# A hybrid trunk layer on one core: first norm summed by TensorE, filter network started earlier, one ScalarE table set for logarithm and exponential

## Chip, core and metric

The kernel runs on one core of a Trainium2 chip. The metric is the device time of one execution in microseconds (us). It is written for the engines directly: every engine has its own instruction queue, and semaphores order them. The profile calls TensorE's matmuls PE and its weight loads PEld, VectorE DVE, ScalarE ACT, GpSimd POOL and SyncE SP.

## What is computed

Two layers (DEPTH = 2) of a trunk, over 512 latent and 128 context tokens (T = 640 columns), with D_MODEL = 1024. The parts that the change touches:

```python
def _rmsnorm(x, w):
    xf = x.astype(jnp.float32)
    y = xf * lax.rsqrt(jnp.mean(xf * xf, axis=-1, keepdims=True) + EPS)
    return (y * w.astype(jnp.float32)).astype(x.dtype)

def _hyena_filters(seq, w1, b1, w2, b2, w3, freq):
    ...
    h = jnp.sin(fr * (z @ w1.astype(f32) + b1.astype(f32)))
    h = jnp.sin(fr * (h @ w2.astype(f32) + b2.astype(f32)))
    h = h @ w3.astype(f32)
    deltas = jnp.abs(jnp.linspace(HY_SLOW_DECAY, HY_FAST_DECAY, HY_W, dtype=f32))
    return h * jnp.exp(-t[:, None] * jnp.tile(deltas, 2))

def _trunk_layer(x, p, l, cond, ctx):
    ...
    h = _rmsnorm(x, p['norm_mix_w'][l]) * (1.0 + sc_a) + sh_a
    mix, new_ctx = _mixer_sublayer(h, p, l, ctx)
    x = x + gt_a * mix
    h = _rmsnorm(x, p['norm_mlp_w'][l]) * (1.0 + sc_m) + sh_m
    x = x + gt_m * (jnp.square(jax.nn.relu(h @ p['mlp_w1'][l])) @ p['mlp_w2'][l])
    return x, new_ctx
```

The mixer has four branches (latent attention A, gated delta rule B, Hyena long convolution C whose filters come from `_hyena_filters`, differential attention D). Each has further RMS or L2 norms. A final norm follows the second layer.

## The kernel before

The activations stay transposed in SBUF: `x` and `h` are 8 chunks (KC = 8) of 128 features by 640 tokens. Every 1024-wide product is split into a high and a low part: weights come by DMA into a ring of four slots (`w_ring`), ScalarE rounds them into `w_high` (`high_part`, `win_high`), GpSimd subtracts to get `w_low` (`low_part`), and TensorE multiplies high by high, high by low and low by high. The order on every engine is written out by hand.

**The start.** SyncE issues the loads of the condition, of the first constants, of `x`, of two blocks of the input projection, and then of four 2 MB groups of modulation weights (`w_early`, groups 0 to 3); group 2 waits for the first projection block, group 3 for the second. Projection blocks 2 and 3 are issued when groups 0 and 1 have landed. ScalarE squares the eight chunks of `x` into `h` (`square`). VectorE adds each squared chunk to the next, in a chain of seven adds. TensorE then sums over the partitions with a matrix of ones (`first_norm_sum`), and ScalarE makes the reciprocal root as exp(-0.5 ln(mean + eps)) (`root`). From there on `first_projection` goes through the four groups: `rows(g)` multiplies the condition by a group's weights, VectorE copies the result, `turn(g)` turns it into columns, VectorE forms scale and shift, then the chunks of `h` are scaled, split and multiplied into blocks 0 and 1 of the input projection (`high_products`, `low_products`).

**The filter network of layer 0.** It has three small products. `filter_first` multiplies positions by `w1`; VectorE reduces the argument to the sine's range in six instructions (`sin_arg(l, 1, ...)`), ScalarE takes the sine (`sine(1)`), TensorE multiplies by `w2` behind projection block 2, the same again (`sin_arg(l, 2, ...)`, `sine(2)`), and then `windowed` multiplies five tiles by `w3`, two tiles behind block 3 and three behind block 4; VectorE multiplies each by its window. Between these VectorE runs a short convolution of three instructions for every projection block (`conv`), and ScalarE evacuates each block from PSUM (`evac_conv`), which also rounds the weights of the block two later. All of this is in program order on each queue, so that a late sine argument holds what stands behind it.

**The copy of x.** `x`'s SBUF space is used for other data in the mixer, so GpSimd stores `x` to a DRAM tensor `x_kept` when all chunks have been scaled, and brings it back chunk by chunk in `merge`'s last eight steps, each as soon as the merged chunk is taken.

**ScalarE's tables.** Logarithm and exponential stand in different function tables as the program is built: there is an ACT_TABLE_LOAD ahead of the logarithm and another one ahead of the exponential in every root. A load is placed ahead of the last wait of the instruction that it serves. `stay_busy` gives TensorE 31 products without use while the roots of the layers' later norms are made.

## Time and profile before

| | us |
|---|---|
| median of 3 runs | 2681.46 (2676.06 to 2685.02) |
| profiled execution, its own time | 2686.07 |
| its span | 2684.3 |
| PE busy | 2565.2 (96%) |
| PEld busy | 2397.3 (89%) |
| DVE busy | 1533.7 (57%) |
| ACT busy | 981.1 (37%) |
| POOL busy | 695.6 (26%) |

The profiled execution is one of several, and 1.8 us of its time lie outside its span. A busy PE in this table counts a matmul from its start to its modelled end, at whichever clock it ran.

### The profile page before, as it was taken

Reading aid. Unit: us, or ns where it says so; the run is one execution under the profiler, and the core shown is the slowest. Engines: PE = TensorE matmul, PEld = TensorE weight load, DVE = VectorE, ACT = ScalarE, POOL = GpSimd, SP = SyncE. Lnnn points to the kernel's source line nnn. Section 1 sums busy time; section 2 is a strip of 40 time slices with the busy share of each in tenths; the row PEclk is TensorE's granted clock in tenths of the full one; section 3 lists DMA queues with packets and bytes.
Section 4 is the critical chain, followed back from the end, with each engine's and each line's share of the span. In section 5 each row is a group of like instructions: output and inputs, shape, how many; then the busy total and the mean of one; then the engine's idle time right before and its main releaser. Section 6 shows DMA issues by size and latency. Waiting matters only on the chain.

```text
span 2684.3 us, 53995 instructions
## 1 busy us (share of the span) xinstructions
PE 2565.2 (96%) x23046; PEld 2397.3 (89%) x23046; DVE 1533.7 (57%) x2507; ACT 981.1 (37%) x1590; POOL 695.6 (26%) x528
## 2 busy tenths in 40 slices
PE   6998999999999999999999989999999999999997
PEld 5788897999999999999987888878898998999997
DVE  6666634546676636355475675355565957355364
ACT  4251033334432534253442511443344226253352
POOL 2322122332244220211223311323222431211202
PEclk9999999999999999999999999999999999999999
DMA  9010011633333223223431100234332422122222
GB/s 360 31 56 3 3 50 68 196 109 105 109 132 122 67 91 110 88 94 97 143 140 32 48 3 3 70 132 131 116 112 96 167 81 71 64 86 75 82 73 79
DMA packets 74713, 248.21 MB, mean 92 GB/s; under 512 B 8948, under 2 KB 21412, under 8 KB 73200
## 3 DMA queue, kind: packets, MB, share of 16 engines
q1 hardware_dynamic: 71264, 220.32, 24.3%
q0 software_dynamic: 3216, 24.49, 2.5%
q8 instruction: 183, 3.00, 0.5%
q14 instruction: 50, 0.41, 0.1%
HBM read 227.56 MB, written 17.21 MB: 91 GB/s over the span
## 4 chain that ended last, share of the span: by engine, by line
PE 77%; DVE 12%; ACT 6%; issue 4%; DMA 1%; POOL 1%; DVEq 0%; ACTq 0%; SPq 0%; POOLq 0%
PE ps_dense L1067 29%; PE ps_dense L1075 13%; PE ps_aux L1067 4%; PE ps_dense L1984 4%; PE ps_dense L1750 3%; PE ps_dense L1988 2%; PE ps_aux L1514 2%; DVE rs L3126 2%; PE ps_dense L1831 1%; PE ps_aux L1807 1%; PE ps_aux L1500 1%; PE ps_dense L1819 1%; PE ps_aux L1466 1%; ACT w_high L2510 1%; ACT flow L2520 1%
## 5 line engine op out<-in xcount | busy, mean ns | idle before, releaser
L880 POOL TENSOR_TENSOR w_low<-w_ring,w_high 128x256 fp32r<-128x256 f32 (+1 forms) x338 | 538.9, 1610 | 1417.9 <-ACT w_high L2130 1406.2
L2130 ACT ACTIVATE w_high<-w_ring 128x1024 fp32r<-128x1024 f32 x198 | 210.0, 1061 | 368.7 <-PE ps_dense L1067 260.3
L1067 PE MATMUL ps_dense<-z_both,w_high 128*128 128x320 f32 x2048 | 312.5, 310 | 0.0
L1067 PEld LDWEIGHTS ps_dense<-z_both,w_high 128*128 128x128 f32 x2048 | 302.6, 188 | 2.1 <-issue 1.6
L1075 PE MATMUL ps_dense<-h_high,w_high 128*128 128x320 f32 x1024 | 240.7, 316 | 8.0 <-DVE x_res L3148 3.5
L3292 DVE SCALAR_TENSOR_TENSOR x_res<-ps_dense,mod,x_res 128x320 f32<-128x320 f32 (+2 forms) x192 | 72.6, 434 | 292.5 <-PE ps_dense L1067 292.5
L1075 PE MATMUL ps_dense<-h_high,w_low 128*128 128x320 f32 x1024 | 233.1, 309 | 0.0
L1075 PE MATMUL ps_dense<-h_low,w_high 128*128 128x320 f32 x1024 | 232.5, 308 | 0.0
L1067 PE MATMUL ps_dense<-h_high,w_high 128*128 128x320 f32 x864 | 206.1, 320 | 11.4 <-ACT h_high L2177 8.5
L1067 PE MATMUL ps_dense<-h_low,w_high 128*128 128x320 f32 x864 | 191.4, 313 | 0.3 <-DVE h_low L2681 0.3
L1075 PEld LDWEIGHTS ps_dense<-h_high,w_high 128*128 128x128 f32 x1024 | 168.3, 188 | 15.4 <-issue 13.2
L1075 PEld LDWEIGHTS ps_dense<-h_low,w_high 128*128 128x128 f32 x1024 | 171.2, 188 | 0.0
L1075 PEld LDWEIGHTS ps_dense<-h_high,w_low 128*128 128x128 f32 x1024 | 170.9, 188 | 0.0
L1067 PEld LDWEIGHTS ps_dense<-h_high,w_high 128*128 128x128 f32 x864 | 147.0, 193 | 25.3 <-issue 13.5
L1067 PE MATMUL ps_dense<-z_both,w_low 128*128 128x320 f32 x1024 | 160.6, 309 | 0.0
L1067 PEld LDWEIGHTS ps_dense<-z_both,w_low 128*128 128x128 f32 x1024 | 152.8, 188 | 0.0
L1067 PEld LDWEIGHTS ps_dense<-h_low,w_high 128*128 128x128 f32 x864 | 145.5, 192 | 0.9 <-DVE h_low L2681 0.5
L1067 PE MATMUL ps_dense<-h_high,w_low 128*128 128x320 f32 x864 | 145.2, 310 | 0.0
L3170 DVE TENSOR_REDUCE att_s<-ps_aux 128x1 f32<-128x640 f32 (+1 forms) x120 | 82.2, 713 | 92.5 <-PE ps_aux L1807 51.9
L1067 PEld LDWEIGHTS ps_dense<-h_high,w_low 128*128 128x128 f32 x864 | 131.9, 189 | 0.0
L1984 PE MATMUL ps_dense<-h_low,w_high 128*128 128x320 f32 x392 | 117.1, 310 | 0.0
L1984 PE MATMUL ps_dense<-h_high,w_high 128*128 128x320 f32 x336 | 102.6, 317 | 10.1 <-DVE flow L3438 10.0
(529 smaller groups left out, 5126.2 us busy)
## 6 DMA issues: line engine op xcount, KB each, us to landing
w_ring<-in_w_mlp SPq DMA_DIRECT2D x128, 512.0 KB, 3.5
w_ring<-in_w_late SPq DMA_DIRECT2D x64, 640.0 KB, 4.0
w_ring<-in_w_gate SPq DMA_DIRECT2D x64, 512.0 KB, 5.2
w_ring<-in_w_in SPq DMA_DIRECT2D x48, 512.0 KB, 3.3
w_ring<-in_w_out SPq DMA_DIRECT2D x16, 512.0 KB, 3.4
w_ring<-in_w_early SPq DMA_DIRECT2D x16, 512.0 KB, 3.3
arena<-in_w_early SPq DMA_DIRECT2D x3, 2048.0 KB, 16.5
arena<-in_dft POOLq DMA_DIRECT2D x2, 2944.0 KB, 13.4
```

The source lines that it names most:

```text
L880: last = g.tensor_tensor(w_low[:, n % 2, k:k + step], ring[:, slot, k:k + step, :], w_high[:, n % 2, k:k + step].bitcast(F32), ALU.subtract)
L1067: last = mm(out[:, s, 0:HALF], w_[:, par_, k, :], x_[:, k, s * HALF:(s + 1) * HALF], start=first, stop=final)
L1075: last = mm(out[:, s, 0:HALF], w_[:, par_, k, :], x_[:, k, s * HALF:(s + 1) * HALF], start=k == 0 and x_ is x_high and w_ is w_high, stop= ...
L1466: return mm(psA[to, 2 * i, u * 64:(u + 1) * 64], lt[s % 3][rows(r), d, hh, rows(r)], mv, start=True, stop=True)
L1514: last = mm(out, wm[i][at, u], mv, start=not moved, stop=True)
L1750: last = mm(out[:, s, 0:HALF], w_[:, k, :], x_[:, k, s * HALF:(s + 1) * HALF], start=n == 0 and k == 0, stop=n == 2 and k == 1)
L1984: mm(out, w_[:, k // 2, k % 2], src[:, k], start=fresh and k == 0 and n == 0, stop=False, skip_group_check=True)
L1988: last = mm(out, rest[:, k // 2, k % 2], b_high[:, k], start=False, stop=k == 3, skip_group_check=True)
L2130: a(w_high[:, n % 2], ring[:, j, 0:KC, :], ACT.Copy).then_inc(w_high_in.sem, 1)
L3126: link(v.scalar_tensor_tensor(out=product, in0=w[:, a:b], scalar=1.0, in1=cond_c[:, a:b], op0=ALU.mult, op1=ALU.mult, accum_out=total))
L3170: v.tensor_reduce(small_[:, 2 * m, u:u + 1], src, AX.XY if len(src.shape) == 3 else AX.X, ALU.max, negate=True).then_inc(negmax.sem, 1)
L3292: last = v.scalar_tensor_tensor(out=dst[:, p:q], in0=ps, scalar=gate[:, s:s + 1], in1=dst[:, p:q], op0=ALU.mult, op1=ALU.add)
```

## The change

It has four parts. (1) VectorE sums the squared chunks 0 to 5 only; TensorE adds chunks 6 and 7 and the sum in its accumulation, after 12 products without use that start when `x` has landed. (2) `filter_first` of layer 0 goes ahead of the products of chunks 6 and 7, its three small loads are issued by GpSimd when `rows(0)` is done (before: `rows(1)` done and group 3 landed), and in layer 0 the second sine argument and the second sine go ahead of convolution 1 and of the evacuation of block 2. (3) In layer 0 `x_kept` is not written, and `x` comes back from the kernel's input. (4) A table set that holds logarithm and exponential is loaded by name in every root (`both_tables`), and the separate load ahead of the exponential is gone. `stay_busy` has 28 products.

```diff
-        squares_in = signal("squares_summed", 2 * (KC - 2), KC - 1)
+        squares_in = signal("squares_summed", 2 * (KC - 2), KC - 3)
...
-        x_out = signal("x_kept_out", 1, 0, 16)
+        x_out = signal("x_kept_out", 1, -1, 16)
...
-            held(pool, block_done.sem, RING + 2 * RING)
-            held(pool, ring_in[1].sem, 32)
+            held(pool, block_done.sem, RING + RING)
             filter_positions()
             first_par = ins["par"][DEPTH - 1]
             for a, b in ((PAR["w1"][0], PAR["w3"][0]), (PAR["lam"][0], PAR_W)):
                 pool.dma_start(par[:, a:b], first_par[:, a:b]).then_inc(z_in.sem, 16)
+            held(pool, ring_in[1].sem, 32)
...
-                held(pool, *x_scaled.nth(l, KC))
-                pool.dma_start(x_kept, x[:]).then_inc(x_out.sem, 16)
+                if l:
+                    held(pool, *x_scaled.nth(l, KC))
+                    pool.dma_start(x_kept, x[:]).then_inc(x_out.sem, 16)
...
-                    pool.dma_start(x[:, d], x_kept[:, d]).then_inc(x_back.sem, 16)
+                    pool.dma_start(x[:, d], (x_kept if l else ins["x"])[:, d]).then_inc(x_back.sem, 16)
...
             def first_norm_sum():
-                pe.wait_ge(squares_in.sem, KC - 1)
-                for a, b in SEGS:
-                    last = mm(psD[:, 0, a:b], c_("ones"), h[:, KC - 1, a:b], start=True, stop=True)
+
+                pe.wait_ge(x_in.sem, 16)
+                for _ in range(12):
+                    mm(psA[:, 2, 0:P], c_("ones"), c_("ones"), start=True, stop=True)
+                for n, (c, event) in enumerate(((KC - 2, x_squared.nth(0, KC - 1)), (KC - 1, x_squared.nth(0, KC)),
+                                                (KC - 3, (squares_in.sem, KC - 3)))):
+                    pe.wait_ge(*event)
+                    for a, b in SEGS:
+                        last = mm(psD[:, 0, a:b], c_("ones"), h[:, c, a:b], start=n == 0, stop=n == 2)
                 last.then_inc(sumsq_done.sem, 1)
...
-                for _ in range(31):
+                for _ in range(28):
                     mm(psA[:, 2, 0:P], c_("ones"), c_("ones"), start=True, stop=True)
...
+                pe.wait_ge(first_scale.sem, 2 * RING)
+                filter_first(0)
                 high_products(KC - 2)
                 high_products(KC - 1)
                 for b in range(2):
                     low_products(KC - 2, b)
                     low_products(KC - 1, b).then_inc(block_done.sem, 1)
-                    if b == 0:
-                        filter_first(0)
...
+            def both_tables():
+
+                nc.scalar.preload_act_table_set("natural_log_exp_and_others")
+
...
-                        nc.scalar.preload_act_table(ACT.Ln)
+                        both_tables()
...
-                    if n == 2:
+                    if n == 1 + (l > 0):
                         sine(2)
...
                 evac_conv(l, 11)
+                both_tables()
                 length_ln(l, 2)
...
             def diff_root(l):
 
+                both_tables()
                 act.wait_ge(*do_sum.nth(l, 1))
...
             a(cond_t[:], cond[:], ACT.Tanh, scale=0.5).then_inc(g_tanh.sem, 1)
+            both_tables()
             act.wait_ge(x_in.sem, 16)
...
-                    if n == 2:
+                    if n == 1 + (l > 0):
                         sin_arg(l, 2, flat, p_("hb2", r), r)
                     conv(l, n, dst, w, bias)
                     if n == 3:
                         dve.wait_ge(const_rest_in.sem, 48)
-                        dve.wait_ge(*x_out.nth(l, 1))
+                        if l:
+                            dve.wait_ge(*x_out.nth(l, 1))
                         dve.wait_ge(*dft_in.nth(l, 1))
...
-            for c in range(1, KC):
+            for c in range(1, KC - 2):
```

TensorE's first rows in the program, before: the sum over the partitions (L1113), the condition by weight group 0 (L1101), its turn (L1171).

```order
L1113 MATMUL ps_dense<-h_norm,con_and_par 128x512
L1113 MATMUL ps_dense<-h_norm,con_and_par 128x128
L1101 MATMUL ps_aux<-arena,cond_pad 32x128 x32
L1171 MATMUL ps_aux<-con_and_par,bout 128x8
L1101 MATMUL ps_aux<-arena,cond_pad 32x128 x32
```

The same place in the changed program, where L1115 are the products without use and L1120 the sum.

```order
L1115 MATMUL ps_aux<-con_and_par 128x128 x12
L1120 MATMUL ps_dense<-h_norm,con_and_par 128x512
L1120 MATMUL ps_dense<-h_norm,con_and_par 128x128
L1120 MATMUL ps_dense<-h_norm,con_and_par 128x512
L1120 MATMUL ps_dense<-h_norm,con_and_par 128x128
L1120 MATMUL ps_dense<-h_norm,con_and_par 128x512
L1120 MATMUL ps_dense<-h_norm,con_and_par 128x128
L1102 MATMUL ps_aux<-arena,cond_pad 32x128 x32
L1178 MATMUL ps_aux<-con_and_par,bout 128x8
```

Two sums and the 12 products stand ahead of what was the first row. The next place is on VectorE, between the first sine argument and the second one; before, with the end of the first argument (L2710), the convolutions 0 and 1 (L2692 to L2696, twice) and the start of the second argument (L2702).

```order
L2710 TENSOR_SCALAR arena<-arena 64x640
L2692 TENSOR_SCALAR arena<-stage,con_and_par 128x642
L2694 SCALAR_TENSOR_TENSOR arena<-stage,con_and_par,arena 128x642
L2696 SCALAR_TENSOR_TENSOR arena<-stage,con_and_par,arena 128x642
L2692 TENSOR_SCALAR arena<-stage,con_and_par 128x642
L2694 SCALAR_TENSOR_TENSOR arena<-stage,con_and_par,arena 128x642
L2696 SCALAR_TENSOR_TENSOR arena<-stage,con_and_par,arena 128x642
L2702 TENSOR_SCALAR arena<-ps_aux,con_and_par 64x640
```

And in the changed program, where the lines of the argument are L2718 to L2726 and those of the convolution L2708 to L2712.

```order
L2726 TENSOR_SCALAR arena<-arena 64x640
L2708 TENSOR_SCALAR arena<-stage,con_and_par 128x642
L2710 SCALAR_TENSOR_TENSOR arena<-stage,con_and_par,arena 128x642
L2712 SCALAR_TENSOR_TENSOR arena<-stage,con_and_par,arena 128x642
L2718 TENSOR_SCALAR arena<-ps_aux,con_and_par 64x640
```

Convolution 1 now stands behind the second argument. The third place is ScalarE's start; before, with the condition's tanh (L2615), the squares (L2142), the first rounded weights (L2622) and the root (L2155, L2156).

```order
L2615 ACT_TABLE_LOAD
L2615 ACTIVATE cond_t<-cond_s 128x16
L2142 ACTIVATE h_norm<-x_res 128x640 x8
L2622 ACTIVATE w_high<-w_ring 128x1024 x2
L2155 ACT_TABLE_LOAD
L2155 ACTIVATE rs<-ps_dense,con_and_par 128x640
L2156 ACT_TABLE_LOAD
L2156 ACTIVATE rs<-rs 128x640
```

And now, where L2108 is the load by name.

```order
L2630 ACT_TABLE_LOAD
L2630 ACTIVATE cond_t<-cond_s 128x16
L2108 ACT_TABLE_LOAD
L2153 ACTIVATE h_norm<-x_res 128x640 x8
L2638 ACTIVATE w_high<-w_ring 128x1024 x2
L2166 ACTIVATE rs<-ps_dense,con_and_par 128x640
L2167 ACTIVATE rs<-rs 128x640
```

One load has moved ahead of the squares, and the other one is gone.

## Rows read from the trace of the kernel before

**Rows 1.** The page's chain of work that ended last.

```profile
PE 77%; DVE 12%; ACT 6%; issue 4%; DMA 1%; POOL 1%; DVEq 0%; ACTq 0%; SPq 0%; POOLq 0%
```

**Rows 2.** Timeline of the start: start us, us, engine line op, [idle before <-releaser].

```profile
10.92 5.12 ACT L2142 ACTIVATE h_norm<-x_res 128x640 f32<-128x640 f32 x8 [8.28 <-DMA x_res<-in_x]
12.32 6.74 DVE L3526 TENSOR_TENSOR h_norm<-h_norm 128x640 f32<-128x640 f32 x7 [9.26 <-ACT h_norm L2142]
...
19.20 2.47 PE L1113 MATMUL ps_dense<-h_norm,con_and_par 128*128 128x512 f32 x4 [19.20 <-DVE h_norm L3526]
...
21.61 2.68 PE L1101 MATMUL ps_aux<-arena,cond_pad 128*32 128x128 f32 x64
21.72 0.79 ACT L2155 ACTIVATE rs<-ps_dense,con_and_par 128x640 f32<-128x640 f32 x1 [2.48 <-PE ps_dense L1113]
...
28.39 0.53 PE L1067 MATMUL ps_dense<-h_high,w_high 128*128 128x320 f32 x2 [1.34 <-ACT h_high L2177]
```

**Rows 3.** Timeline: what tells when the weight groups had landed.

```profile
18.83 5.26 SPq L790 DMA_DIRECT2D w_ring<-in_w_in  x2
...
35.15 0.54 POOL L892 DMA_DIRECT2D arena<-in_dft  x1 [11.41 <-DMA bout<-in_w_early]
...
38.37 1.95 PE L1101 MATMUL ps_aux<-bout,cond_pad 128*32 128x128 f32 x64
```

**Rows 4.** Timeline at the first filter product (L1136).

```profile
47.65 1.29 PE L1136 MATMUL ps_aux<-arena,con_and_par 33*64 33x512 f32 x4
47.75 0.44 ACT L2108 ACTIVATE stage<-ps_dense 128x320 f32<-128x320 f32 x1 [2.44 <-PE ps_dense L1067]
...
48.45 1.07 ACT L2130 ACTIVATE w_high<-w_ring 128x1024 fp32r<-128x1024 f32 x1
...
49.07 0.94 DVE L2702 TENSOR_SCALAR arena<-ps_aux,con_and_par 64x640 f32<-64x640 f32 x1 [2.75 <-PE ps_aux L1136]
...
49.58 0.56 PE L1067 MATMUL ps_dense<-h_high,w_high 128*128 128x320 f32 x2
```

**Rows 5.** Timeline from the second filter product (L1257) to the last tiles (L1246).

```profile
56.80 1.29 PE L1257 MATMUL ps_aux<-arena,con_and_par 64*64 64x512 f32 x4
...
61.76 0.93 DVE L2702 TENSOR_SCALAR arena<-ps_aux,con_and_par 64x640 f32<-64x640 f32 x1
...
68.01 0.74 ACT L2183 ACTIVATE arena<-arena 64x640 f32<-64x640 f32 x1 [5.58 <-DVE arena L2710]
...
68.89 3.75 PE L1246 MATMUL ps_aux<-con_and_par,arena 64*128 64x512 f32 x4 [3.58 <-ACT arena L2183]
...
74.60 0.69 DVE L2722 TENSOR_TENSOR arena<-ps_aux,arena 128x512 f32<-128x512 f32 x1
...
82.13 2.84 PE L1246 MATMUL ps_aux<-con_and_par,arena 64*128 64x512 f32 x6
```

**Rows 6.** Busy time by stretch: PE, PEld, DVE, ACT, POOL, PE's granted clock, DMA, GB/s.

```profile
72.60:77.70 5.10, 5.10 (x20) 5.10 (x20) 4.77 (x8) 0.00 (x0) 0.48 (x1) 0.50 0.00 0
```

**Rows 7.** The second instruction of a convolution, both layers: duration ns min/median/max, starts.

```profile
L2694 DVE SCALAR_TENSOR_TENSOR arena<-stage,con_and_par,arena x24: 886/889/3120, 55.6 to 1508.6; 128x642 f32<-128x642 f32 x24
```

**Rows 8.** The norm ahead of layer 0's MLP, and all loads ahead of a root's exponential.

```profile
L2156 ACT ACT_TABLE_LOAD  x5: 1283/1283/1283, 22.5 to 2672.4; - x5
...
893.91 1.24 PE L1119 MATMUL ps_dense<-h_norm,con_and_par 128*128 128x512 f32 x4
...
897.25 7.09 PE L1128 MATMUL ps_aux<-con_and_par 128*128 128x128 f32 x62
...
905.16 0.53 PE L1067 MATMUL ps_dense<-h_high,w_high 128*128 128x320 f32 x2 [0.82 <-ACT h_high L2177]
```

**Rows 9.** Timeline: what waits for differential attention's root in layer 0.

```profile
754.20 0.83 PE L1750 MATMUL ps_aux<-con_and_par_reused,w_proj_high 128*128 128x320 f32 x4 [0.54 <-issue]
```

**Rows 10.** Timeline: the first gate's tanh in layer 0's attention.

```profile
465.02 0.70 ACT L2363 ACTIVATE stage<-ps_dense 128x640 f32<-128x640 f32 x1 [1.71 <-PE ps_dense L1101]
```

**Rows 11.** The line that brings x back (L1038), min/median/max of both layers' 16 transfers.

```profile
DMA to landing us min/median/max: 3.2/3.3/5.0
```

More of the change, by code:

```diff
@@ L2443, in mla @@
                 act.wait_ge(*stored.nth(l, 1))
+                both_tables()
                 for n, wd in enumerate((256, 128)):
@@ L2602, in mlp_group @@
                 if at_end:
-                    nc.scalar.preload_act_table(ACT.Ln)
+                    both_tables()
                     for m in (KC - 2, KC - 1):
@@ L2615, in _ @@
             a(cond_t[:], cond[:], ACT.Tanh, scale=0.5).then_inc(g_tanh.sem, 1)
+            both_tables()
             act.wait_ge(x_in.sem, 16)
```

## The prediction

> **What bounds the kernel now.** I read the page first: TensorE carries 77% of the chain that ended last, VectorE 12%, ScalarE 6% [rows 1]. So an edit on another engine counts only where TensorE waits for it, and I looked at the four kinds of places that the change touches. At the start TensorE has nothing until 19.20, when VectorE's seven adds are through; its sum takes 2.47 and the weight rows begin at 21.61 [rows 2]. In the filter network of layer 0 TensorE stands 3.58 for the second sine, and then runs slowly [rows 5]: its granted clock is 0.50, the 1.2 GHz level, until 77.7 [rows 6]. In every norm outside the mixer ScalarE's logarithm, load and exponential are in series with TensorE, which has only idle products [rows 8]. In the mixer TensorE mostly works beside the roots.
>
> **The start.** Removed: two adds of the seven, 6.74/7 = 0.96 each, so the sum of chunks 0 to 5 is there at 12.32 + 5 x 0.96 = 17.1 instead of 19.1. Added: 12 products without use and two sums. TensorE can begin at about 10.95, when x has landed [rows 2]. One idle product takes 7.09/31 = 0.23 at full speed [rows 8], so 12 take 2.8, or 5.5 at half speed: they end by 16.5 at the latest, and the square of chunk 6 is there at about 15.4, that of chunk 7 at 16.0. A sum takes 1.24 where TensorE is warm [rows 8] and took exactly twice that, 2.47, in this place [rows 2]; the 64 weight rows behind it took 2.68 against 1.95 later [rows 2, 3], so the clock rose among them, after some 4 us of work. Starting 8 us earlier, the clock should rise within the 12 products. Then three sums of 1.24 end at about 19.3; were all at half speed, they would end at 16.5 + 3 x 2.47 = 23.9. Before it was 21.67. The load ahead of the first exponential (1.28) is gone too [rows 8], so the reciprocal root comes earlier by more than the sum does, and is not what comes last.
>
> The gain of 2.4 meets the DMA. Group 0 had landed at 18.83, group 1 at about 18.83 + 5.26 = 24.1 or just before, since these issues wait for them; group 3 at 35.15 [rows 3]. The rows of group 0 go from 19.3 to 21.3, those of group 1 from 24.0 to 25.9, and the first products of block 0 follow at 25.9 instead of 28.39 [rows 2]: 2.5 earlier. The last group's rows then come up at 38.37 - 2.5 = 35.9, 0.7 behind their landing [rows 3]. The three small loads that GpSimd now issues before group 3 is in can eat that 0.7, hardly more. I take **-2.5**, with ends -3.2 (down to the landing at 35.15) and +2.2 (all sums at half speed).
>
> **The filter of layer 0.** Moving `filter_first` ahead is not free. Its product takes 1.29, and block 0 was evacuated at 47.75, just as that product began [rows 4]; now block 0 ends behind it, and ScalarE's evacuation and the rounding of block 2's weights (48.45 to 49.52) move by about 1.2. TensorE began block 2 at 49.58, right on them [rows 4], so it begins block 2 at 50.8: **+1.2** (bounds +0.6 and +1.3). What it buys: VectorE waited 2.75 for the first argument [rows 4] and now starts it at about 46.4, so the first sine is no danger for the second product, which comes 7.2 behind block 2's start (56.80 against 49.58 [rows 4, 5]), at 58.0, ending at 59.3. The second argument, now ahead of convolution 1, starts at 59.4 instead of 61.76, and the sine ended 6.99 after the argument's start (61.76 to 68.75 [rows 5]). It ends at 66.4 at the latest. TensorE comes from block 3 at 65.3 + 1.3 = 66.6 (it stood 3.58 before 68.89 [rows 5]). So the wait is gone, and with it the low clock: two tiles took 3.75 and take 2.84 x 2/3 = 1.9 warm [rows 5]. Block 4 lasted from 72.6 to 82.1, 9.5, and at full speed it takes what block 2 took, 7.2 [rows 4, 5, 6]. TensorE is done with block 4 at 66.6 + 1.9 + 7.2 = 75.7 instead of 82.13: -6.4, with the 1.2 in it.
>
> What is late next is VectorE: it windowed the first tile at 74.60 [rows 5] with the convolutions 2 and 3 behind the sine, 6.6 after 68.01, and now has convolution 1 there too: three instructions of at most 0.89, so 2.7, or 4.9 if one of them is held as the longest here, 3.12 [rows 7]. From 65.7, the start of the new sine, this gives 65.7 + 6.6 + 2.7 = 75.0 to 77.2 for the first tile, and twice 0.69 more for the second. TensorE wants the second at about 76.7. I put 0.7 on it (bounds 0 and 3). Net **-5.7**; ends -7.0 and -2.5. The evacuation of block 2 behind the second sine (65.7 + 0.7) leaves block 4's weights 2 us to be rounded and ready by 68.5, enough.
>
> **No copy of x in layer 0.** 2.6 MB less to DRAM in a stretch where VectorE's wait for it is ahead of the first tile; before, the sine was later than the copy. Cost and gain 0 here; without this part the filter's gain could be held by it. The way back is from another DRAM tensor with the same shape and the same number of transfers, 3.3 each [rows 11]: 0.
>
> **Table loads.** Each root outside the mixer loses one load of 1.283 and a gap of about 0.02, in series: two norms ahead of MLPs, layer 1's first norm, the final norm. The first of the kernel is counted above. The cover is long enough: 28 idle products end 3 x 0.23 = 0.7 earlier, and the first real product comes 1.3 earlier than 905.16, where it stood idle for 0.82 [rows 8], so 0.2 of idle remains. 4 x 1.30 = **-5.2**, bounds -5.2 and -3.5. In the mixer: behind the scan's inputs one load goes ahead of the exponential and one comes back ahead of the next tanh, 0; at the roots of the scan and of latent attention TensorE works beside them, 0; a load comes in ahead of the first gate's tanh, but ScalarE stood there for 1.71 [rows 10], more than 1.28, so 0 (1.3 if that cover were gone). At differential attention's root TensorE stood 0.54 before the product that waits for the exponential [rows 9], which ends 1.28 earlier, twice in the kernel: up to -1.1, and I take **-0.5**, since VectorE and GpSimd bound that stretch next.
>
> The Trainium skill ("ScalarE: Activation LUTs", section "What ACT_TABLE_LOAD costs") puts a switch at about 2.66: the load and a drain of 1.38 behind it. In this trace the next instruction starts within 0.02 of the load's end, so the trace does not show the drain. By the page the four loads would be worth 10.6 in place of 5.2, and the sum 5.4 more.
>
> **The sum.** -2.5 - 5.7 - 5.2 - 0.5 = -13.9. Against the profiled execution, 2686.07, that is 2672.2. The median of the three runs is 4.6 lower than it, 2681.46, and I forecast the new median from there: 2681.5 - 13.9 = **2667.6**.
>
> **The rivals.** (a) *TensorE stays slow at the start*: the clock rises late, or falls again in the 2 us between the turn of group 0 and the landing of group 1 (it fell around the wait of 3.58, and did not fall at 1.34 [rows 2, 5]). Then the start gives between +2.2 and -1, the total about -10: 2671. (b) *The filter's gain goes into the next wait*: the tiles wait for VectorE for 3 us or more, and where the wait is long enough the clock falls there. Then the filter gives -2.5 or less, the total -8 to -10: 2672. (c) *A table switch costs more than its row shows* (the page's rule, worked out as a mechanism here: a pause of 1.4 in ScalarE behind each load): nothing in the trace shows it; 2662. (d) *Slower*: `in_x` is read more slowly than `x_kept`. GpSimd issues these loads one behind the other and waits for each, with the subtraction for the next block queued behind the wait, and TensorE behind that. The loads took 3.3 [rows 11], hidden in the step of a gate. It decides when one takes longer than a step of some 9 us; with 12 us each, 8 x 3 = 24 less 13.9 gives 2692. Nothing speaks for it, the sizes are the same. (e) *The filter part doesn't do what it says*, because the second argument waits for TensorE's second product in any case; that is true from 55 to 59.4, but the argument still starts 2.4 earlier and has no convolution ahead. Covered by (b).
>
> **Chances.** Forecast, all parts about as summed (2663 to 2671): 0.60. (a) 0.15, (b) 0.16, (c) 0.04, (d) 0.02, and 0.03 for a new median that moves by more than the parts do, since the three runs shown lie 9 us apart. The range, 2660 to 2675, holds the forecast, (a), (c) and most of (b). A measurement tells this kernel from no change at about 0.3%, 8 us, which is 2673.4: faster by more than that 0.82, within 0.3% 0.15, slower 0.03.
>
> **What would show it.** In the changed profile: TensorE busy from about 11; sum done at about 19.3, with the last sums near 1.24; weight rows of group 1 straight at the landing, near 24; block 0's first products near 26; no wait of over 1 us for ScalarE's sine, and a granted clock of 1.00 through 65 to 80 at both tile groups; a wait of about 1 us at the start of block 2. 7 loads fewer in all, none between a root's logarithm and its exponential, and TensorE's first product behind each norm 1.3 nearer to its sum. The prediction is wrong if the sums run at half speed, if the second tile group waits for VectorE for more than 3 us, or if the norms' products don't move with the exponential.

## The result, and the profile after

The changed kernel takes 2660.58 us, median of 4 runs (2659.78 to 2663.39); the kernel before, on the same chip, 2678.76 (2675.22 to 2685.02, 4 runs). The ratio is 0.9928 with a 95% interval of 0.9907 to 0.9949: 19.3 us less, between 13.7 and 24.9; the medians lie 18.2 apart. Forecast were 13.9 less. The changed kernel's time lies 0.6 inside the lower edge of the range (2660 to 2675), 7.0 under the forecast of 2667.6. The profiled execution took 2661.06, with a span of 2659.2 against 2684.3 before.

The page of the changed kernel, the chain of work that ended last, its shares by engine (the view of [rows 1]), and from the list of DMA queues the one that brings instructions:

```profile
PE 79%; DVE 10%; ACT 5%; issue 3%; DMA 1%; POOL 1%; SPq 0%; DVEq 0%; ACTq 0%; POOLq 0%
...
q8 instruction: 183, 3.00, 0.5%
```

VectorE's and ScalarE's shares fell by 2 and 1 points, and so did "issue".

Timeline of the start of the changed kernel, TensorE alone (start us, us, line, form, idle before and what ended it; the view of [rows 2]):

```profile
10.84 4.28 PE L1115 MATMUL ps_aux<-con_and_par 128*128 128x128 f32 x24 [10.84 <-DMA x_res<-in_x]
15.27 3.51 PE L1120 MATMUL ps_dense<-h_norm,con_and_par 128*128 128x512 f32 x12 [0.15 <-ACT h_norm L2153]
18.71 1.95 PE L1102 MATMUL ps_aux<-arena,cond_pad 128*32 128x128 f32 x64
...
23.58 3.34 PE L1102 MATMUL ps_aux<-arena,cond_pad 128*32 128x128 f32 x64 [2.04 <-DMA arena<-in_w_early]
26.85 0.79 PE L1068 MATMUL ps_dense<-h_high,w_high 128*128 128x320 f32 x2
```

The sums run at full speed (3.51 for three, 1.17 each) and end at 18.8, 0.5 ahead of the forecast. Then TensorE waits 2.04 for the second group of weight rows, and those rows take 3.34 where the first group's took 1.95. The stretches of the same profile say why (busy time of PE, PEld, DVE, ACT, POOL, then PE's granted clock, DMA share, GB/s); the second row is where the filter's first tiles are multiplied (the view of [rows 6]):

```profile
24.00:27.20 3.20, 3.20 (x58) 2.82 (x50) 2.23 (x7) 2.38 (x4) 0.00 (x0) 0.50 1.03 416
65.00:72.00 7.00, 7.00 (x40) 5.62 (x39) 6.89 (x5) 1.77 (x4) 5.25 (x2) 1.00 0.23 75
```

The clock had gone to 0.50, the 1.2 GHz level, right behind the wait. Block 0's first products come at 26.85, 1.54 earlier than before and not 2.5. That is this profile: in the changed kernel's second one (e12 below) the same wait is 1.40, the clock stays up, the rows take 1.95, and block 0 comes at 25.59:

```profile
23.71 1.95 PE L1102 MATMUL ps_aux<-arena,cond_pad 128*32 128x128 f32 x64 [1.40 <-DMA arena<-in_w_early]
25.59 0.56 PE L1068 MATMUL ps_dense<-h_high,w_high 128*128 128x320 f32 x2
```

The filter network in layer 0, same timeline and columns (the views of [rows 4, 5]):

```profile
43.18 1.29 PE L1143 MATMUL ps_aux<-arena,con_and_par 33*64 33x512 f32 x4
49.46 0.56 PE L1068 MATMUL ps_dense<-h_high,w_high 128*128 128x320 f32 x2 [1.27 <-ACT w_high L2141]
56.68 1.29 PE L1264 MATMUL ps_aux<-arena,con_and_par 64*64 64x512 f32 x4
65.14 1.98 PE L1253 MATMUL ps_aux<-con_and_par,arena 64*128 64x512 f32 x4
...
74.75 1.12 PE L1253 MATMUL ps_aux<-con_and_par,arena 64*128 64x512 f32 x2 [0.41 <-DVE arena L2741]
76.15 1.55 PE L1253 MATMUL ps_aux<-con_and_par,arena 64*128 64x512 f32 x3 [0.27 <-DVE arena L2741]
```

The wait of 3.58 is gone, the tiles take 1.98 for 3.75, and the price of the moved product stands where it was put: 1.27 of idle time ahead of block 2.

The norm ahead of layer 0's MLP, all engines (the view of [rows 8]):

```profile
877.15 6.42 PE L1135 MATMUL ps_aux<-con_and_par 128*128 128x128 f32 x56
877.36 0.79 ACT L2166 ACTIVATE rs<-ps_dense,con_and_par 128x640 f32<-128x640 f32 x1 [1.44 <-PE ps_dense L1129]
878.18 0.74 ACT L2167 ACTIVATE rs<-rs 128x640 f32<-128x640 f32 x1
...
883.78 0.39 PE L1068 MATMUL ps_dense<-h_high,w_high 128*128 128x320 f32 x1 [0.21 <-ACT h_high L2188]
```

The exponential starts 0.03 behind the logarithm, and the first product comes 6.63 behind the first idle one (877.15 to 883.78); before it was 7.91. That is the load, 1.28, and the idle rest is the 0.2 that was forecast.

### The profile page after: what moved, and what is told of

Same layout as the page of the kernel before. It is cut to its first block, busy times and chain, and to the rows that moved or that the text cites. A ratio compares the mean times of both kernels' runs of the same rounds, so it can differ in the third digit from the quotient of the medians.

```text
span 2659.2 us, 54007 instructions
## 1 busy us (share of the span) xinstructions
PE 2559.3 (96%) x23060; PEld 2391.8 (90%) x23060; DVE 1530.1 (58%) x2505; ACT 972.3 (37%) x1583; POOL 693.0 (26%) x527
## 4 chain that ended last, share of the span: by engine, by line
PE 79%; DVE 10%; ACT 5%; issue 3%; DMA 1%; POOL 1%; SPq 0%; DVEq 0%; ACTq 0%; POOLq 0%
PE ps_dense L1068 29%; PE ps_dense L1076 14%; PE ps_dense L1991 5%; PE ps_aux L1068 5%; PE ps_dense L1757 3%; PE ps_dense L1995 2%; PE ps_aux L1521 2%; PE ps_dense L1838 1%; PE ps_aux L1814 1%; PE ps_aux L1507 1%; PE ps_dense L1826 1%; DVE rs L3143 1%; PE ps_aux L1473 1%; ACT flow L2535 1%; ACT w_high L2525 1%
## 5 line engine op out<-in xcount | busy, mean ns | idle before, releaser
L1068 PEld LDWEIGHTS ps_dense<-h_high,w_low 128*128 128x128 f32 x864 | 132.0, 189 | 0.0
## 6 DMA issues: line engine op xcount, KB each, us to landing
arena<-in_w_early SPq DMA_DIRECT2D x3, 2048.0 KB, 18.2
```

What stands on the lines that cost most here:

```text
L1068: last = mm(out[:, s, 0:HALF], w_[:, par_, k, :], x_[:, k, s * HALF:(s + 1) * HALF], start=first, stop=final)
```

## Where the rest came from: pauses in TensorE's instruction stream

I followed the same instructions through both profiles. Behind the filter (TensorE's first product with 32 output rows, at 92.12 before, at 85.28 now; from here on the milestone) the changed kernel was 6.8 ahead; the two scans of the delta rule (branch B) I had not priced at all. I measure a scan from the product that always stands behind a pause of 1.17 to 1.19 (L1356; L1363 now) to the first product of `ps_dense<-stage,bout`, in before from 179.52 to 315.96 in layer 0 and from 1506.83 to 1639.56 in layer 1. These stretches in before, in the changed kernel, and in the kernel before profiled a second time (columns as above; layer 0, then layer 1):

```profile
179.52:315.96 136.44, 121.23 (x3009) 113.06 (x3009) 90.61 (x145) 28.76 (x52) 26.49 (x30) 0.96 0.04 11
1506.83:1639.56 132.73, 119.12 (x3008) 111.31 (x3008) 90.44 (x145) 28.76 (x52) 26.48 (x30) 0.97 0.04 11
```

```profile
172.66:300.29 127.63, 115.71 (x3009) 108.15 (x3009) 90.31 (x145) 28.89 (x52) 26.52 (x30) 1.00 0.04 11
1483.76:1615.84 132.08, 119.58 (x3009) 111.76 (x3009) 90.47 (x145) 28.89 (x52) 26.51 (x30) 0.97 0.04 11
```

```profile
178.73:311.47 132.74, 118.40 (x3008) 110.05 (x3008) 90.48 (x145) 28.75 (x52) 26.53 (x30) 0.99 0.04 11
1499.55:1632.47 132.92, 119.42 (x3008) 111.62 (x3009) 90.50 (x145) 28.76 (x52) 26.52 (x30) 0.97 0.04 11
```

The work is the same, 3009 products, and layer 0's took 8.8 less. Two things differ: how often the granted clock fell (3 times in 179 to 316 before, never in the changed kernel, once in the second profile), and pauses in the middle of a run of equal products, which wait for nothing that the profile shows. One of them in before, the same place in its second profile, and in the changed kernel, where the 64 products run through (timeline, TensorE alone):

```profile
291.67 1.59 PE L1514 MATMUL ps_aux<-arena 64*64 64x64 f32 x47
294.12 0.68 PE L1514 MATMUL ps_aux<-arena 64*64 64x64 f32 x17 [0.86 <-issue]
```

```profile
289.92 0.68 PE L1514 MATMUL ps_aux<-arena 64*64 64x64 f32 x17 [1.14 <-issue]
```

```profile
278.60 2.06 PE L1521 MATMUL ps_aux<-arena 64*64 64x64 f32 x64
```

What these pauses have in common shows when one counts. TensorE's products (x) from the start to just before two of them in the kernel before:

```profile
0.00:236.00 236.00, 203.66 (x2116) 177.60 (x2116) 151.74 (x233) 87.43 (x145) 67.79 (x56) 0.97 0.34 127
0.00:245.20 245.20, 211.57 (x2368) 184.90 (x2368) 158.15 (x244) 89.68 (x148) 71.08 (x59) 0.97 0.32 123
```

A product is two instructions (the weight load and the multiplication), and a wait that doesn't fit into one is an instruction of its own: 57 such waits stand ahead of the first pause, 65 ahead of the second. So the pauses stand at instruction 2 x 2116 + 57 = 4289 and 2 x 2368 + 65 = 4801: 512 apart, both 193 over a multiple of 256. The changed kernel's whole program has 2 x 23060 + 886 = 47,006 such instructions (before: 2 x 23046 + 886); in 3.00 MB of instruction traffic that is 64 bytes each, and a packet, 3.00 MB / 183 = 16 KB, holds 256. The runs below confirm that this queue is TensorE's and a packet 256 of its instructions: with 512 more instructions ahead (e7, e8) it has 185 packets, with 192 more (e10) 184, with 64 more (e9) still 183. In all 17 profiles of this study every pause inside the scans of over 0.25 us, 80 of them, stands 192 or 193 over a multiple of 256 (two counted 195). The packets themselves agree: ahead of each of the twelve pauses in the two profiles of before one had landed, and the products went on 1.19 to 1.50 after it (for the one above, landed at 292.93, products at 294.12). In all 80 it is 1.19 to 1.77. So a pause is not at a place in the algorithm but at a place in the packet; my reading, which fits all of this but which no run shows apart, is that TensorE there runs through short products faster than the packets come. Code put in ahead moves all later pauses to other products. The change puts 64 instructions ahead of layer 0's scan (12 idle products and 4 more sums, of two passes each); 12 of them are taken back at each of the two norms between the scans (3 idle products of two passes), so it is 40 in layer 1.

## The experiments

Fifteen runs follow; e5 is the kernel before and e12 the changed kernel, unchanged. A table first, from their profiles: "shift" is by how many instructions TensorE's code stands further than in before (modulo 256), then pauses of over 0.25 and their sum, falls of the clock, and the length of the scan.

| profile | layer 0: shift | pauses, sum | falls | us | layer 1: shift | pauses, sum | falls | us |
|---|---|---|---|---|---|---|---|---|
| before | 0 | 4, 3.33 | 3 | 136.4 | 0 | 2, 1.77 | 2 | 132.7 |
| e5 (before again) | 0 | 4, 2.77 | 1 | 132.7 | 0 | 2, 1.22 | 2 | 132.9 |
| e2 (filter) | 0 | 4, 3.02 | 1 | 132.7 | 0 | 2, 1.97 | 2 | 133.6 |
| e1 (tables) | 0 | 4, 3.03 | 1 | 133.2 | -24 | 3, 3.38 | 0 | 132.7 |
| e7 | 512 = 0 | 3, 1.51 | 1 | 130.9 | 0 | 3, 2.19 | 2 | 134.1 |
| e8 | 512 = 0 | 3, 2.34 | 1 | 132.0 | -24 | 5, 3.92 | 1 | 134.0 |
| e10 | 256 = 0 | 3, 2.09 | 2 | 133.5 | -24 | 4, 3.29 | 0 | 132.2 |
| e4 | 48 | 1, 0.37 | 0 | 128.4 | 48 | 4, 2.89 | 1 | 132.0 |
| e6 | 48 | 3, 1.18 | 1 | 130.7 | 48 | 3, 1.82 | 1 | 131.2 |
| changed | 64 | 0 | 0 | 127.6 | 40 | 3, 1.53 | 2 | 132.1 |
| e12 (changed again) | 64 | 0 | 1 | 129.4 | 40 | 3, 1.89 | 1 | 131.5 |
| e13 | 64 | 2, 0.60 | 0 | 127.9 | 40 | 3, 1.76 | 1 | 131.3 |
| e15 | 64 | 1, 1.17 | 1 | 131.1 | 40 | 3, 1.56 | 2 | 132.1 |
| e3 (start) | 64 | 1, 0.28 | 1 | 129.2 | 64 | 1, 0.36 | 1 | 129.1 |
| e9 | 64 | 2, 1.27 | 1 | 130.5 | 64 | 1, 0.62 | 1 | 129.4 |
| e11 | 64 | 0 | 0 | 127.6 | 64 | 1, 0.36 | 1 | 128.8 |
| e14 | 64 | 0 | 0 | 128.0 | 64 | 2, 1.51 | 0 | 129.0 |

Median of layer 0: 132.7 at a shift of 0 (7 profiles), 128.6 at 64 (8): 4.1 less. Of layer 1: 133.2 at 0 (4), 131.8 at 40 (4), 129.1 at 64 (4). The expectations below count a scan from a later product, 10.0 behind mine in layer 0 and 5.7 in layer 1: their 122 is 132 here. Each profile is of one execution, and not always of a middle one: e6's and e10's were the slowest of their 12.

**The three parts alone, and 12 idle products alone.** e1, e2 and e3 are the kernel before with the lines of the diff that belong to the tables (with the 28 idle products), to the filter, or to the first norm. e4 is the kernel before with

```
             def first_norm_sum():
+                pe.wait_ge(x_in.sem, 16)
+                for _ in range(12):
+                    mm(psA[:, 2, 0:P], c_("ones"), c_("ones"), start=True, stop=True)
```

> The kernel before with only the table part of the change (one table set for logarithm and exponential, 28 idle products for 31). By my sum: four norms give 1.30 each and the roots of differential attention up to 1.1, -5.7 in all, -4 to -6.5. Theory P (what the whole change gained beyond the sum lies in layer 0's mixer, in falls of TensorE's clock and pauses of its instruction stream that depend on where its code stands and when it runs, not in a part): -5.7 outside the mixer, and in the mixer of layer 0 the same number of clock falls and pauses as before, since no TensorE instruction is added ahead of it. Rival S (the tables part is worth more than its rows, by a pause of 1.4 behind each switch): -11.

> The kernel before with only the filter part (first product of the filter and second sine one step earlier, the three small loads before the wait for group 3). By my sum -5.7 plus nothing, -7 to -2.5. The trace of the changed kernel gives -6.7 at the end of block 4 against its start. Theory P: -5 to -7 at 100 us, and the same through layer 0's mixer but for clock falls at other times. Rival S: this part also frees the mixer, so that -12 or more stands behind layer 0.

> The kernel before with only the first norm changed (12 idle products, three chunks summed on TensorE). My sum says -2.5; the trace of the changed kernel has -1.5 at block 0's first product, because the clock falls in a wait of 2.04 before the second group of weight rows. Expected -1.5 at that place. Theory P: TensorE's code stands 16 products later in all that follows, so the pauses in layer 0's delta-rule stretch (236, 245, 294, 303) are gone as in the changed kernel, and behind layer 0 it is -4 to -9. Rival S: -1.5 stays -1.5 to the end.

> The kernel before with 12 idle products ahead of TensorE's first sum and nothing else. At the start the clock should be up when the sum runs, 1.24 for 2.47, but then TensorE waits for the second group of weight rows: 0 to -1.3 at block 0's first product. Theory P: its code stands 12 products later, so the pauses of the delta-rule stretch are gone or elsewhere, and the kernel ends 3 or more us earlier than block 0's gain accounts for. Rival S (position does nothing): 0 to -1.3 to the end.

Against before (2680.46, 29 runs): tables 0.9973 (0.9959 to 0.9987), -7.2 us; filter 0.9986 (0.9974 to 0.9998), -3.8; start 0.9966 (0.9953 to 0.9979), -9.1; 12 idle products 0.9976 (0.9964 to 0.9987), -6.4. The three parts add up to 20.1 against 19.3 for all together, so these runs show no gain that needs two parts; their intervals leave room for some 8 either way. The tables did what their rows said. The start part did not: its profile is only 0.6 ahead of before behind the filter (91.12 against 92.12 and 91.34 in the two profiles of before), yet the kernel is 9.1 faster. e4 does not have the new sums, is 1.3 ahead at the same place (90.44), and gives 6.4. The gain is downstream: at the end of layer 0's scan the profiles of e3 and e4 are 6.0 and 7.5 ahead of the mean of before's two.

**Moving the code, and nothing else.** e5 is before unchanged. e6 and e7 put 12 and 128 products of 64 by 64 ahead of TensorE's first sum, e8 takes 124 of them for the changed kernel's 12 idle ones:

```
+                for _ in range(12):      # 128 in e7, 124 in e8
+                    mm(psA[0:64, 2, 0:64], c_("ones")[0:64, 0:64], c_("ones")[0:64, 0:64], start=True, stop=True)
```

> The kernel before once more, for a second profile of it. Theory P (pauses of TensorE's instruction stream belong to places in its code): the pauses of layer 0's scan at 294 and 303 and of layer 1's at 1564 and 1573 stand at the same instructions again, and the scan takes 122 or more, as in the three profiles with this code position so far (126.4, 123.1, 122.6). Rival R (they are chance): fewer than two of the four come back.

> The kernel before with 12 products of 64 by 64 ahead of TensorE's first sum, while it waits: they end before the sum's inputs are there, so nothing moves at the start; only TensorE's code stands 24 instructions later from there on. Theory P: no pause in layer 0's scan, which takes 117.5 to 119.5 instead of 122.6 to 126.4, and the kernel is 3 to 7 faster. Rival W (the gain of the 12 idle products came from the earlier clock): no change, scan 122 or more.

> The same with 128 products, 256 instructions, which is as much as one 16 KB packet of TensorE's instruction queue holds (64 bytes each). They take some 5 to 8 in the wait of 8 at the start and may warm the clock for the sum. Theory P: packets and code stand to each other as in the kernel before, so the pauses at the two places in layer 0's scan are back, the scan takes 122 or more, and the kernel is 0 to 2 faster than before. Rival R or W: no pauses, as with 12 idle products, 3 to 7 faster.

> The changed kernel with 124 products of 64 by 64 in the place of the 12 idle ones, which puts its code back to the place against the 16 KB packets that it had before the change (256 instructions later). Theory P: the pauses in layer 0's scan are back, the scan takes 122 or more instead of 117.6, and the kernel loses 4 to 8 of its 18, which leaves about the sum of my parts: 2665 to 2669. Rival: it stays at 2660 to 2663 (up to 1.5 for the later sums at the start).

e5: the four pauses are back at the same four instructions of layer 0 (233.6, 242.8, 289.9, 298.4; 3.33 in sum before, 2.77 now), and layer 1's two as well. e6: 0.9982 (0.9972 to 0.9992), -4.8, with its first sum still at half speed (2.50), so the gain does not come from the clock at the start; but I had expected no pause, and there are three short ones in layer 0, whose scan takes 130.7 where I had expected at most 129.5. My count was wrong as well: a product is two passes here, so 12 products are 48 instructions and 128 are 512, which is 0 modulo 256 all the same. e7 and e8 cost far more at the start than I had allowed (their short products took 0.11 a pass, one behind the other: 27.6 and 26.7 in all). Their ratios, 1.0054 (1.0041 to 1.0067) and 1.0043 (1.0028 to 1.0057), say only that, and the times that I had forecast for them missed; what counts is behind it. The milestone of 92.12 stands at 101.36 in e7 and at 106.78 in e8. e7 ends 12.2 later than before (medians) and 9.6 of that is there by the milestone (mean of before's two: 91.73), so nothing is gained behind it. e8 ends 28.8 later than the changed kernel and 21.0 of that is there by then (mean of its two: 85.77): 7.8 are lost behind it, which is what the position should cost. But this takes one profile's milestone from medians of different sessions: going by the two ratios instead (+11.5 and -19.3) it is 9.8, and the intervals leave some 7 either way. The pauses of e8 in layer 0 are at 4801, 5313 and 8129, before's 4289, 4801 and 7617 plus 512: the same products.

**The same with empty instructions.** e9 is before with 64 of them ahead of TensorE's first wait, e10 the changed kernel with 192 there, e11 the changed kernel with 12 ahead of each norm's idle products, e12 the changed kernel unchanged:

```
+                for _ in range(64):      # 192 in e10, 12 in e11
+                    pe.nop().then_inc(held_waits.sem, 1)
```

> The kernel before with 64 empty instructions ahead of TensorE's first wait, where it stands idle for 19: no product added, no clock touched. Theory P, sharpened by the runs so far: all pauses inside runs of small products stood where the count of TensorE's instructions (two for each product record, one for each separate wait) leaves 192 or 193 over a multiple of 256, and the code position that the changed kernel and the start part have in layer 0 is 64 further. So no pause of over 0.45 in either layer's scan, which take 117.5 to 121 and 123 to 126, and the kernel is 4 to 8 faster than before. Rival W (clock, timing or the sums at the start): no change.

> The changed kernel with 192 empty instructions in the same place: with the 64 of the change, 256, the code stands in layer 0 to the packets as in the kernel before; they end before x has landed or take at most 1 or 2 more. Theory P: pauses at the same instructions of layer 0's scan as before the change, scan 122 or more for 117.6, the kernel at 2665 to 2669, 5 to 8 over the changed one. Rival: 2660 to 2662.

> The changed kernel with 12 empty instructions ahead of the 28 idle products of each norm. The change took 3 idle products there, six records and twelve instructions, so its code stands 24 nearer in layer 1's scan than in layer 0's; this puts it back to the position at which the start part alone showed no pause in either layer. Theory P: the two pauses of layer 1's scan (0.73 and 0.51) are gone, that scan takes 123 to 125 for 126.4, and the kernel is at 2656 to 2659. Rival: 2660 to 2662; or worse, if 12 empty instructions delay the idle products.

> The changed kernel once more, in the same conditions as the three others, and for a second profile: 2660 to 2661; no pause in layer 0's scan and the two of layer 1 at the same instructions; the clock's falls in the mixer at other times.

e9 is the cleanest: the start is untouched (its sum begins at 18.87 and takes 2.47), nothing is added but position, and it takes 0.9973 (0.9960 to 0.9985) of before, 7.2 us less, 4.0 to 10.7. Its milestone is at 91.75, before's mean is 91.73. Its scans (columns as above):

```profile
179.15:309.62 130.47, 117.50 (x3008) 109.83 (x3009) 90.36 (x145) 28.86 (x52) 26.48 (x30) 0.99 0.04 11
1497.97:1627.33 129.36, 117.47 (x3009) 109.88 (x3009) 90.44 (x145) 28.83 (x52) 26.50 (x30) 0.99 0.04 11
```

Not all pauses of over 0.45 are gone, though I had said they would be: one of 0.90 and one of 0.62 are left. e10 lost 18.3 by the milestone, where I had allowed 1 or 2, since TensorE's first product came only at 30.89; behind it the kernel is another 4.8 later than e12 (2684.05 against 2660.99), and the pause of 294.12 is back before the last 17 of the 64 products:

```profile
303.77 0.69 PE L1523 MATMUL ps_aux<-arena 64*64 64x64 f32 x17 [0.82 <-issue]
```

e12 came out as expected: no pause in layer 0, layer 1's at the same instructions, the clock's falls elsewhere. e11 gives layer 1 the position of layer 0: 128.8 for 132.1 and 131.5 in its scan, with one pause of 0.36 left. In time it is 2659.65 (6 runs) against e12's 2660.99 (6 runs), the right way but within what runs differ by.

**What was left.** e13 is the changed kernel with the copy of x back; e14 has e11's 12 empty instructions, 10 idle products for 12, and two wide ones in the wait for group 1; e15 has the first filter product back in its old place:

```
                     turn(g)
+                    if g == 0:
+                        for _ in range(2):
+                            mm(psA[:, 2, :], c_("ones"), x[:, 0, 0:512], start=True, stop=True)
```

> The changed kernel with the copy of x in layer 0 put back (start, filter and table parts of the change alone). My sum prices the copy at 0: then 2660 to 2662, and 35.0 to 36.5 from the second window block to the first tiles' end in layer 0 as in the changed kernel (19.4 and 16.6 in its two stretches). Rival: VectorE's wait for the copy comes last once the second sine is early, and the first tile stands 1 to 4 later: 2662 to 2665.

> The changed kernel with 12 empty instructions ahead of each norm's idle products (layer 1's scan without its two pauses, -2 to -3) and, at the start, 10 idle products instead of 12 and two wide products without use behind the turn of group 0, where TensorE waits 2.04 for the second group of weight rows; the count of instructions stays. Theory: the clock fell at 23.9 because of that wait, so with it filled the rows of group 1 take 1.95 instead of 3.34 and block 0's first products follow 0 to 1.3 earlier (they then wait for their chunk, as before the change, where they stood 1.34). The kernel at 2655.5 to 2659. Rival: the clock falls all the same, or does not rise within 10 idle products: 2658 to 2661.

> The changed kernel with the filter's first product back in its old place, the second sine still ahead of convolution 1. I priced its move at +1.2 for block 2's weights, and thought it was needed. In the changed kernel the second sine ends 2.2 before TensorE comes to the tiles, so the move may be unneeded: block 2 begins at 48.2 instead of 49.46, TensorE comes to the tiles at 63.9 instead of 65.14, and no wait for a sine stands there; the milestone at the end of block 4 is 1.2 earlier. Rival: the first sine is now late for the second product (over 0.5 of wait) or the second for the tiles, and the milestone stays or moves later.

e13: 2665.45, 0.9943 (0.9927 to 0.9960). By time alone that is where the rival put it, but the interval does not tell it from the changed kernel's 0.9928 and 0.9934. Its profile speaks for 0: from block 2 to the first tiles it takes 15.68 as in the changed kernel, and TensorE waits 0.41 and 0.27 for VectorE at the second ones, as there; the copy is not what comes last. What its profile loses on e12's is for the most part two falls of the clock behind the scan, at 339 and 425, which cost it 1.6 and 3.1; e15, without the copy, has them at the same products, at 345 and 431, with the same cost. e14: 2658.27, 0.9920 (0.9906 to 0.9935), the fastest version measured, by 2.3 and 2.7 under the changed kernel's two medians, which the intervals do not separate. Layer 1's pauses are not gone, as I had thought: two are left, 1.51 in sum. Its start (timeline, TensorE):

```profile
21.42 1.96 PE L1209 MATMUL ps_aux<-x_res,con_and_par 128*128 128x512 f32 x4
23.57 1.96 PE L1102 MATMUL ps_aux<-arena,cond_pad 128*32 128x128 f32 x64 [0.18 <-DMA arena<-in_w_early]
...
30.28 1.96 PE L1102 MATMUL ps_aux<-arena,cond_pad 128*32 128x128 f32 x64 [0.76 <-DMA arena<-in_w_early]
```

With the wait filled the clock stays up and the rows take 1.96; the next group is then awaited for 0.76, and block 2 begins at 48.74. It begins at 49.46 in the changed kernel's first profile, where the clock fell at the start, and at 48.91 in e12, where it did not: the fall costs 1.3 at block 0 and about half a microsecond at block 2, and filling the wait gains no more than that, since the DMA takes back the rest. e15 shows what the moved product buys (timeline, TensorE, at the two tile groups):

```profile
73.72 1.12 PE L1253 MATMUL ps_aux<-con_and_par,arena 64*128 64x512 f32 x2 [1.19 <-DVE arena L2741]
77.26 3.78 PE L1253 MATMUL ps_aux<-con_and_par,arena 64*128 64x512 f32 x4 [2.42 <-DVE arena L2741]
```

Block 2 did begin 1.3 earlier than at its earliest in the changed kernel (47.66), but VectorE has its first argument later (47.16, changed 44.83) and TensorE waits 3.6 for it at the tiles, where the clock then falls. The milestone is at 90.42 for 85.28 and 86.26, and its only execution took 2672.78. The price of 1.2 was well paid.

## Why the prediction was wrong, and what of it held

**"In the mixer 0", the step that failed.** I summed only edits on the path and took the rest of TensorE's time as fixed: apart from -0.5 at differential attention's root the mixer stood in the sum with 0. It is not fixed: the change moves all later code by 64 and 40 instructions against its packets. Layer 0's scan is 4.1 shorter at the changed position, layer 1's 1.4 (medians of the table). TensorE also loses 0.6 to 1.6 between 450 and 500, a stop that stands in all profiles with a shift of 0 and in none with 48 or 64; I have not found its cause, it ends with a VectorE instruction. These are some 6.3 that the prediction did not have. The direct test, e9, gives 7.2 for moved code alone, with both layers at 64. That the change moved the code to a better place, and not to a worse one, is luck: nothing in its design or in the prediction chose the 64 instructions, and e10, the same kernel with 192 more, loses about 5 behind the start.

Followed product by product, as means of the two profiles of each kernel, the changed one is ahead by 6.0 at the milestone, 12.1 at the end of layer 0's scan, 14.3 behind the stop just named, 16.6 behind the norm of layer 0's MLP, 18.2 behind layer 1's first norm, 18.7 at the end of layer 1's scan, 18.5 behind the norm of its MLP, and 19.8 at the end. Of this 12.5 stand where I had put a price (6.0 at the start and in the filter, 5.1 at four norms, 1.4 at the two roots of differential attention), against the 13.9 of my sum. The rest, 7.3 in these profiles, is the mixer. So the sum of the parts alone was near, and a little high; the total was low for a term that I had put at 0 without a reason.

**The start, -2.5 forecast, 1.2 to 1.6 found with the filter part, 0.6 without.** The sums were right to 0.5. Block 0 came at 25.45 to 25.93, where I had put it (25.9), in e11 to e15. Rival (a), the clock falling in the wait for group 1, came about in the changed kernel's first profile (the row at 0.50 above), in e15 and in e3, behind waits of 2.04, 2.04 and 3.50, and not in e11, e12 and e13, behind 0.92, 1.40 and 1.84. The wait is as long as the DMA makes it. Wrong was what I made of block 0's gain: TensorE waits again at the next group, so I had priced one landing and there were several. Block 2 begins at 50.62 in e2, which has the filter part alone, and at 49.46, 48.91 and 48.94 in the changed kernel's two profiles and e11; of the profiles in which the clock stays up at the tiles, the milestone is at 86.44 in e2 and at 85.28 and 84.81 in the changed kernel's first and e11. The start part alone, e3, where group 1 landed late and block 0 came at 28.44, is 0.6 ahead.

**The filter, -5.7 forecast, -5.3 found** (e2's milestone, 86.44 against 91.73; its time says 3.8, 0.5 to 7.0). All its steps stand in the profile: +1.27 ahead of block 2 for 1.2; no wait for a sine; both tile groups begun at full speed; VectorE next, with 0.41 and 0.27 for the 0.7. Rival (b) has a small part: in e12, e13 and e14, though not in the first profile, e2 or e11, the clock fell behind these two waits, and from the second tile group to the milestone it took 1.5 to 3.1 longer (12.0, 13.7 and 13.7 for 10.5).

**The copy of x, 0 forecast, none seen in the profile** (e13; its time leaves room for up to some 9). **The table loads, -5.2 forecast, -5.1 found**: from the first idle product to the first real one 6.63 for 7.91 at layer 0's MLP, 6.70 for 7.98 at layer 1's first norm, 6.63 for 7.90 at its MLP, and 1.28 less at the final norm; 28 loads for 35. At differential attention's root the stop of 0.54 is gone (timeline of the changed kernel, TensorE):

```profile
733.82 0.76 PE L1757 MATMUL ps_aux<-con_and_par_reused,w_proj_high 128*128 128x320 f32 x4
734.42 0.74 PE L1757 MATMUL ps_aux<-bout_low,w_proj_high 128*128 128x320 f32 x4
```

The step from the product ahead of it to the root's first is 0.86 or 0.85 in both profiles of before and in e9, and 0.15 in the changed kernel and in e1, in both layers: 1.4 in all for the -0.5. Rival (c), a switch that costs more than its row, fell with the norms' rows, 1.28 each; e1's time, -7.2 (3.5 to 11.0), would alone not rule out its -11. By the Trainium skill ("ScalarE: Activation LUTs", section "What ACT_TABLE_LOAD costs") it would have been 2.66 a switch; the norm's two intervals, 7.91 and 6.63, don't show the rest. Rival (d) has nothing for it.

Open stays why the packet's place is 193, and which of these places pauses in a given run and for how long (at a shift of 64 some show none, some one of 1.17): I know no more than that they come where products are short. Pauses and falls of the clock both differ between the positions, and I had no run that changed one without the other. The table parts them for layer 0: its 17 lengths are 127.65 plus 1.22 for each microsecond of pause plus 1.59 for each fall, all within 0.5 (a fit by least squares). Between the means at 0 and at 64, which are 4.2 apart, that makes 2.6 for the pauses (2.59 against 0.42) and 1.5 for the falls (1.4 against 0.5). Whether the falls belong to the position is not shown: they come at other products in each execution, 10 outside the last stretch in the first profile of before, 6 in that of the changed kernel. In layer 1 such a sum fits worse, to within 1.0. The 1.17 to 1.19 ahead of each layer's scan is in every profile at any shift, so it is something else.

## What to carry to other kernels

Where an engine runs through thousands of short instructions, their position in the program is a variable of its own: a few instructions put in ahead moved this kernel by 7 us of 2680, more than most edits here were worth. So an edit's worth is its change in the profile's stretch, not the difference of two times, and a control with as many empty instructions tells the two apart, as e9 does. And when a wait is filled, price what the engine behind it waits for next (here the DMA's groups) before counting the gain.

## What the runs showed of the hardware that I had not expected

- TensorE's instructions arrive while the program runs, in packets of 16 KB or 256 instructions, 183 of them here; in the scans' runs of short products TensorE stands up to 1.55 for one (e1, layer 1), in all 80 pauses of over 0.25 at the same place of the packet, give or take two instructions.
- An empty instruction that raises a semaphore is not free: with 192 ahead of it TensorE began at 30.89, 0.16 each from the start of the span at most; with 64 it was on time for its sum at 18.87.
- Products of 64 by 64 one behind the other did not raise the clock: after 27.6 us of them e7's sum took 2.50, where 4.28 us of 128 by 128 products in the changed kernel left it at 1.2 a sum.
- Products of 64 by 64 took six times as long at e7's start as in the scan: 0.11 a pass against 0.018 (64 in 1.16). A factor of two in that may be the clock, which in e7 was still at half speed for the sum behind them (2.50). Besides, e7's all use one quarter of the array and write one output, and the scan's go over all four quarters; what each of these costs, no run shows apart.
